# Four-tap convolutions moved from VectorE to GpSimd, and one modulation group from the input stage to the output projection

## The chip, the cores and the metric

The kernel runs on one core of a Trainium2 chip. The metric is the device time of one execution in microseconds (us); the time before is the median of three runs, 1684.27 us (1683.55 to 1684.93). Profiles come from one further execution of the same program.

The engines in the text: TensorE (PE) multiplies matrices into PSUM, VectorE (DVE), ScalarE (ACT) and GpSimd (POOL) work element by element, SyncE (SP) only issues DMAs. Each runs its own instructions in order, and they wait for each other by semaphores. All data is float32.

## What is computed

One layer of a hybrid backbone on 256 tokens and 256 context tokens of width 2048. What matters here:

```python
sh1, sc1, gt1, sh2, sc2, gt2 = adaln(c, w_mod[l], b_mod[l])     # silu(c) @ w_mod + b_mod, 6 x 2048
hx = modulate(rms_norm(x, g_mix[l]), sh1, sc1)                  # the same for the context with c_ctx
x_pool, x_u, x_v, x_lru, x_lg, x_q, x_k, x_val = jnp.split(hx @ w_in[l], 8, axis=-1)
...
def centred_depthwise_conv(z, w, b):                            # CONV_W = 4 taps, 512 channels
    zp = jnp.pad(z, ((0, 0), (left, CONV_W - 1 - left), (0, 0)))
    out = zp[:, 0:L] * w[0] + b
    for k in range(1, CONV_W):
        out = out + zp[:, k:k + L] * w[k]
    return out
...
# rg_lru: r, i = sigmoid(block-diagonal products of z), a = exp(-8 r softplus(-lam)),
# b = sqrt(1 - a^2) * i * z, a scan over the tokens, forward and backward
y_lru = (hx_f + hx_b) * gelu(x_lg)
x_mixed = x + gt1 * merge_branches(hx, [y_pool, y_sgu, y_lru, y_na], w_branch[l], w_gate[l], w_out[l])
hx2 = modulate(rms_norm(x_mixed, g_ffn[l]), sh2, sc2)
x = x_mixed + gt2 * swiglu(hx2, ...)
```

## The kernel before

**Pieces.** The large weights come in pieces of 512 KB (256 rows by 512 columns) through a ring of four buffers. For each piece SyncE issues the DMA into RAW (L274) once VectorE has done with the piece four earlier, ScalarE rounds it to HI (`high`, L428) once TensorE has done with the piece four earlier, VectorE makes the rest LO = RAW - HI (`low`, L735), and TensorE multiplies HI and LO with both parts of the activations in three passes (L1279 to L1281, in the input stage partly L1251 to L1253). A piece is 12 matmuls of 512 columns where the tokens are the rows.

**The order of the rest.** Pieces are numbered by w. ScalarE and VectorE call `high(w)` or `low(w)` and then `straight(w)`, TensorE multiplies piece w and then calls its own `straight(w)`; these hold, at fixed w, all small work of the branches. Pieces 16 to 63 belong to the input projection, 64 to 95 to the gates of the first pass, 96 to 103 to its branch products. Then a loop makes three more passes of 40 pieces, then come 32 pieces of the output projection, then the feed-forward stage.

**The recurrent branch** has four groups g at LRU_AT = 71, 77, 83, 88. For A = LRU_AT[g]: VectorE convolves at w = A - 3 (L991, L994: one tensor_scalar and three scalar_tensor_tensor over 512 columns, 256 context and 256 x tokens) from LP into one of two rows Z; TensorE makes four float32 products of Z after piece A (L1480, L1481); ScalarE takes sigmoids at A + 4 (L575, L576), tanh and exp at A + 5 (L582, L583), a square root at A + 7 (L587) and the rounded result at A + 9 (L590); VectorE works at A + 6 (L957 to L960, semaphore lru_w), at A + 8 (L966 to L979, with the scans) and at A + 10 (L820). On ScalarE a `high` stands between each two of these steps, on VectorE a `low`.

**The modulation.** The last four of the six vectors are 16 groups of 512 columns, each 16 tiles of w_mod (128 x 512, 256 KB), loaded by GpSimd's queue (L392) and added up by VectorE (`mod_tile`, L832 and L834), then turned by TensorE (`mod_turn`) and read (`mod_columns`, L841, L843). Groups 0 to 2 are early, one tile per piece at w = 24 to 71 with the two rows MR; groups 3 to 11 are in the loop, three per pass at its w = 4 to 35 with the four rows MR4; groups 12 to 15 are in the feed-forward stage. Between groups 8 and 9 GpSimd's queue loads x again (L401, two DMAs of 1 MB in rows of 8 KB). JUNK is a 512-column scratch row that lies in the attention's space and is otherwise used for squares much later.

Of the kernel before, what the change touches and what calls it, by code (L numbers as in the profile page):

```python
# [31 lines left out]
T = 256  # L32
# [61 lines left out]

MOD2_0, EARLY, MOD_TILES = 24, 3, 3 * KT
MOD_AT = [[t for t in range(MOD_TILES) if 4 + t * 32 // MOD_TILES == w] for w in range(BLK)]
# [30 lines left out]
def build(nc, x, c, ctx, c_ctx, w_mod, b_mod, g_mix, g_ffn, g_final, w_in, w_pool, pool_scale,  # L127
# [3 lines left out]
    with ctxs:  # L131
# [217 lines left out]
        def _(pool):  # L349
# [45 lines left out]
            with pool.Fori(0, EARLY) as g:  # L395
                mod_group(g, MR, 2, "mod_landed")
            pool.wait_ge(s("branches_made"), 1)
            with pool.Fori(EARLY, 9) as g:
# [326 lines left out]
        def _(dve):  # L725
# [119 lines left out]
            def straight(w):  # L845
                if MOD2_0 <= w < MOD2_0 + EARLY * KT:
                    mod_tile((w - MOD2_0) // 16, (w - MOD2_0) % 16, ACCM[:, (w - MOD2_0) // 16 % 2, :])
                if w in (47, 63):
                    mod_columns((w - 47) // 16, 0)
                if w == 20:  # L850
# [99 lines left out]
                for g in range(G4):  # L950
# [29 lines left out]
                    if w == LRU_AT[g] + 10:  # L980
                        split_low("lru_hi", g + 1, Y[:, 8 + g, 1, :], HS, Y[:, 8 + g, 0, :], "lru_lo")
                if w + 3 in LRU_AT:

                    g = LRU_AT.index(w + 3)
                    z = Z[:, g % 2, :].rearrange("p (s t) -> p s t", s=2)
                    dve.wait_ge(s("win_read"), 4)
                    if g == 0:
                        dve.wait_ge(s("pooled"), 1)
                    if g >= 2:
                        dve.wait_ge(s("lru_w"), 2 * (g - 1))  # L990
                    own.did(ts(z, LP[:, g, :, 0:T], PB[:, PB_CW + g:PB_CW + g + 1], PB[:, PB_CB + g:PB_CB + g + 1], ALU.mult, ALU.add))  # L991
                    for k in range(1, CONV):
                        own.wait()
                        i = stt(z, LP[:, g, :, k:k + T], PB[:, PB_CW + 4 * k + g:PB_CW + 4 * k + g + 1], z, ALU.mult, ALU.add)  # L994
                        if k < CONV - 1:
                            own.did(i)
                        else:
                            i.then_inc(s("conv"), 1)

            def merge(f, n, b):  # L1000
# [22 lines left out]
            dve.wait_ge(s("lru_lo"), 4)  # L1023
            own.did(dve.tensor_copy(ACCB[:, 2, :], ACCM[:, 0, :]))
            own.wait()
# [3 lines left out]
            with dve.Fori(1, 4) as f:  # L1029
                own.enter(f, 1, 3)  # L1030
                for w in range(BLK):
                    low(f * BLK + (MIX0 + w), w % 4)
                    for t in MOD_AT[w]:
                        mod_tile(f * 3 + t // KT, t % KT, ACCB[:, t // KT, :])
                    if w in MOD_READ_AT:
                        mod_columns(f * 3 + MOD_READ_AT.index(w) - 1, 4)
                    if w == 1:
                        merge(f - 1, 2, 0)
                    if w == 3:
                        merge(f - 1, 3, 2)  # L1040
                    if w == 37:
                        merge(f, 0, 0)
                    if w == 39:
                        merge(f, 1, 2)
                own.leave(1, 3)
# [26 lines left out]
            for n in range(4):  # L1072
                for j in range(8):
# [6 lines left out]
                    if 8 * n + j == 4:  # L1080
                        gate1_spread()
                    if 8 * n + j == 17:
                        mod_columns(11, 6)
                    if n and j == 3:
# [157 lines left out]
        def _(pe):  # L1242
# [175 lines left out]
            def straight(w):  # L1418
                if w in (44, 60):

                    g = (w - 44) // 16
                    pe.wait_ge(s("win_read"), (5, 7)[g])
                    mod_turn(g, ACCM[:, g % 2, :], 0)
                if w in (47, 63):
                    pe.wait_ge(s("mod_read"), (w - 31) // 16)
                if w == 34:
# [45 lines left out]
                for g in range(G4):  # L1472
                    if w == LRU_AT[g]:
                        pe.wait_ge(s("conv"), g + 1)
                        pe.wait_ge(s("pool_lo"), 4)
# [78 lines left out]
            with pe.Fori(1, 4) as f:  # L1554
                base = MIX0 + f * BLK
                for n in range(NB):
# [4 lines left out]
                    for w in gate_group(base, n):  # L1561
                        if w == MG_TURN_AT:
                            pe.wait_ge(s("mg_set"), f)
                            merged_turn(f - 1)
                        if w in MOD_TURN_AT:

                            i = MOD_TURN_AT.index(w) - 1
                            pe.wait_ge(s("mod_read"), f * 3 + i)
                            mod_turn(f * 3 + i, ACCB[:, i % 3, :], 4)
                for n in range(NB):  # L1570
# [6 lines left out]
            def gate1_spread():  # L1577

                pe.wait_ge(s("gate1_diag"), 1)
                pe.wait_ge(s("mg_lo"), 4)  # L1580
                pe.wait_ge(s("mod_read"), 11)
                for n in range(4):
# [3 lines left out]
            def xm_turn(n):  # L1586
# [4 lines left out]
                else:  # L1591
                    pe.wait_ge(s("xmt_set"), n - 1)
                if n == 1:
                    pe.wait_ge(s("mod_read"), 12)
                for k in range(4):
# [5 lines left out]
            for n in range(4):  # L1601
# [4 lines left out]
                for j in range(8):  # L1606
# [8 lines left out]
                    if 8 * n + j == 12:  # L1615
                        pe.wait_ge(s("gate1_rows"), 2)
                        mod_turn(11, ACCB[:, 2, :], 6)
                    if n and j == 3:
# [127 lines left out]
```

## Time and profile before

| | |
|---|---|
| median of three runs | 1684.27 us |
| the profiled execution | 1683.08 us |
| its span in the trace | 1681.4 us |
| mean granted clock of TensorE | 0.989 of full speed |
| PE busy | 1627.3 us (97%) |
| DVE busy | 1095.1 us (65%) |
| ACT busy | 733.1 us (44%) |
| POOL busy | 159.2 us (9%), DMA issue alone |
| DMA | 389.09 MB, 231 GB/s on average |

The page counts an engine as busy while an instruction runs. Matmuls overlap, so a busy TensorE is not one at its peak. A view of waits gives for each group of instructions how long its engine stood idle just before it, and who released it. The view in order of time gives start, duration and, in brackets, the idle time before with its releaser.

### The profile page before, as it was taken

What the parts mean: (1) busy time and instruction counts of PE and PEld (TensorE: products, weight loads), DVE (VectorE), ACT (ScalarE), POOL (GpSimd) and SP (SyncE); (2) the same over time, 40 slices, a digit from 0 to 9 for tenths busy, and PEclk for the clock granted to TensorE, in tenths of its full rate; (3) what the DMA queues carried; (4) which work ended last, traced back from release to release, by engine and by line L of the source; (5) the groups of instructions that cost most, each with busy time, mean ns of one, the idle gap of its engine ahead of it and who ended that gap; (6) DMA issues with size and microseconds to landing.
All of it is one profiled execution on the core that took longest, in us unless ns stands there. A gap on an engine that the chain in (4) does not pass through costs nothing.

```text
span 1681.4 us, 22407 instructions
## 1 busy us (share of the span) xinstructions
PE 1627.3 (97%) x7679; PEld 1321.5 (79%) x7679; DVE 1095.1 (65%) x1218; ACT 733.1 (44%) x798; POOL 159.2 (9%) x294
## 2 busy tenths in 40 slices
PE   5999999999899999999999899999999999999998
PEld 2468889987678888788878688888888888888876
DVE  2424336787788887788856657767665556456477
ACT  4324224547744434344444643444444444444434
POOL 1002011110002212222100001101100000000000
PEclk9899999999999999999999899999999999999999
DMA  9997457664369979989655468778776566666653
GB/s 354 382 366 226 138 150 226 205 218 148 125 206 330 330 261 327 334 283 332 234 187 186 137 204 277 244 236 288 230 275 194 187 193 189 191 189 188 186 163 138
DMA packets 183862, 389.09 MB, mean 231 GB/s; under 512 B 14368, under 2 KB 14608, under 8 KB 182912
## 3 DMA queue, kind: packets, MB, share of 16 engines
q1 hardware_dynamic: 160784, 312.63, 57.2%
q0 software_dynamic: 23024, 75.74, 12.9%
q8 instruction: 34, 0.56, 0.1%
q14 instruction: 20, 0.16, 0.0%
HBM read 385.30 MB, written 3.01 MB: 231 GB/s over the span
## 4 chain that ended last, share of the span: by engine, by line
PE 88%; DVE 4%; ACT 3%; DMA 3%; issue 1%; SPq 0%; DVEq 0%; ACTq 0%; POOLq 0%
PE ps L1279 24%; PE ps L1281 23%; PE ps L1280 23%; PE ps L1251 4%; PE ps L1252 4%; PE ps L1253 4%; PE ps L1247 2%; PE ps L1332 2%; ACT HI L428 1%; DVE LO L735 1%; DMA BR<-in_w_mod 1%; DMA MR<-in_w_mod 1%; DMA RAW<-in_w_branch 1%; PE ps L1441 0%; PE ps L1455 0%
## 5 line engine op out<-in xcount | busy, mean ns | idle before, releaser
L735 DVE TENSOR_TENSOR LO<-RAW,HI 128x1024 fp32r<-128x1024 f32 x504 | 616.2, 1224 | 449.3 <-ACT HI L428 446.8
L428 ACT ACTIVATE HI<-RAW 128x1024 fp32r<-128x1024 f32 x504 | 533.8, 1061 | 790.7 <-PE ps L1281 680.1
L1279 PE MATMUL ps<-HI,H 128*128 128x512 f32 x1904 | 749.9, 394 | 16.1 <-DVE LO L735 10.9
L1281 PE MATMUL ps<-HI,H 128*128 128x512 f32 x1904 | 743.7, 391 | 0.0
L1280 PE MATMUL ps<-LO,H 128*128 128x512 f32 x1904 | 743.3, 390 | 0.0
L1279 PEld LDWEIGHTS ps<-HI,H 128*128 128x128 f32 x1904 | 359.0, 189 | 96.2 <-DVE LO L735 13.1
L1281 PEld LDWEIGHTS ps<-HI,H 128*128 128x128 f32 x1904 | 358.8, 188 | 75.3
L1280 PEld LDWEIGHTS ps<-LO,H 128*128 128x128 f32 x1904 | 359.3, 189 | 74.6 <-issue 1.2
L392 POOL DMA_DIRECT2D BR<-in_w_mod x208 | 112.1, 539 | 749.5 <-DVE BR L834 329.7
L832 DVE SCALAR_TENSOR_TENSOR BR<-BR,SCF 128x512 f32<-128x512 f32 (+1 forms) x195 | 145.7, 747 | 2.8 <-DMA BR<-in_w_mod 1.4
L1251 PE MATMUL ps<-H,HI 128*128 128x256 f32 (+1 forms) x384 | 126.1, 328 | 0.0
L1252 PE MATMUL ps<-H,HI 128*128 128x256 f32 (+1 forms) x384 | 122.5, 319 | 0.0
L1253 PE MATMUL ps<-H,LO 128*128 128x256 f32 (+1 forms) x384 | 122.3, 319 | 0.0
L1251 PEld LDWEIGHTS ps<-H,HI 128*128 128x128 f32 x384 | 73.2, 191 | 21.4 <-issue 16.8
L1253 PEld LDWEIGHTS ps<-H,LO 128*128 128x128 f32 x384 | 73.1, 190 | 5.3
L1252 PEld LDWEIGHTS ps<-H,HI 128*128 128x128 f32 x384 | 73.2, 191 | 4.7
L392 POOL DMA_DIRECT2D MR<-in_w_mod x48 | 26.2, 547 | 190.1 <-DVE ACCM L832 153.3
L1138 DVE TENSOR_TENSOR ATT<-ps,ATT 128x1024 f32<-128x1024 f32 x36 | 43.8, 1218 | 0.0
L1332 PE MATMUL ps<-BR 128*32 128x512 f32 x112 | 24.4, 717 | 18.9 <-DMA BR<-in_w_mod 15.0
L832 DVE SCALAR_TENSOR_TENSOR ACCM<-MR,SCF,ACCM 128x512 f32<-128x512 f32 x45 | 33.6, 747 | 7.4 <-DMA MR<-in_w_mod 7.3
L421 ACT ACTIVATE HI<-RAW 128x1024 fp32r<-128x1024 f32 x16 | 16.8, 1054 | 42.5 <-PE ps L1253 37.9
L731 DVE TENSOR_TENSOR LO<-RAW,HI 128x1024 fp32r<-128x1024 f32 x16 | 19.4, 1223 | 19.9 <-ACT HI L421 19.7
(252 smaller groups left out, 742.3 us busy)
## 6 DMA issues: line engine op xcount, KB each, us to landing
RAW<-in_w_gate SPq DMA_DIRECT2D x128, 512.0 KB, 4.7
BR<-in_w_mod POOLq DMA_DIRECT2D x208, 256.0 KB, 4.5
RAW<-in_w_ffn_gate SPq DMA_DIRECT2D x88, 512.0 KB, 3.8
RAW<-in_w_ffn_up SPq DMA_DIRECT2D x88, 512.0 KB, 3.8
RAW<-in_w_ffn_down SPq DMA_DIRECT2D x88, 512.0 KB, 3.7
RAW<-in_w_in SPq DMA_DIRECT2D x64, 512.0 KB, 4.5
RAW<-in_w_branch SPq DMA_DIRECT2D x32, 512.0 KB, 4.9
RAW<-in_w_out SPq DMA_DIRECT2D x32, 512.0 KB, 4.0
```

What stands on the lines that cost most here:

```text
L392: pool.dma_start(slots[:, k % ring, :], w_mod[0, k * P:(k + 1) * P, bass.ds(2 * D + g * BW, BW)])\
L428: act.activation(HI[:, j % RING, :], RAW[:, j % RING, :], ACT.Copy).then_inc(hi_done, 1)
L735: tt(LO[:, j % RING, :], RAW[:, j % RING, :], HI[:, j % RING, :], ALU.subtract).then_inc(lo_done, 1)
L832: i = stt(acc, src, SCF[:, 0, k:k + 1], acc, ALU.mult, ALU.add)
L1138: tt(flat(ACC[:, n, :]), pair(4 + 2 * (n % 2)), flat(ACC[:, n, :]), ALU.add).then_inc(s("down_read"), 1)
L1251: mm(o, wh, xh, start=first, stop=False, skip_group_check=True)
L1252: mm(o, wh, xl, start=False, stop=False, skip_group_check=True)
L1253: return mm(o, wl, xh, start=False, stop=last, skip_group_check=True)
L1279: mm(o, xh, wh, start=first and t == 0, stop=False, skip_group_check=True)
L1280: mm(o, xh, wl, start=False, stop=False, skip_group_check=True)
L1281: i = mm(o, xl, wh, start=False, stop=last and t == 1, skip_group_check=True)
L1332: m = mm(ps[32 * g:32 * g + 32, 6, :], SCP[:, k, :], mod_raw(p + g // 2)[:, g % 2 * BW:(g % 2 + 1) * BW], start=i % 4 == 0, stop=i % 4 == ...
```

## The change

The convolutions leave VectorE. GpSimd does them, between the early modulation groups and the loop's: per group one tensor_scalar into Z and, for each of the other three taps, a tensor_scalar into the scratch row JUNK and a tensor_tensor that adds it to Z, seven instructions in place of four, each waiting for the one before by the semaphore conv_step. Groups 0 and 1 can run as soon as the attention and the pooling have left JUNK and Z; groups 2 and 3 wait for lru_w as before. TensorE waits for conv_step in place of conv.

EARLY goes from 3 to 2. Group 2 leaves w = 56 to 71, every group of the loop moves on by one place (2 to 10 in place of 3 to 11), and group 11 is added up during the output projection, one tile per piece at its pieces 8 to 23, turned after piece 27 and read at piece 31. The second load of x stands where it did in GpSimd's program, behind group 8, and that group is now the first of the third pass of the loop (the last of the second before).

```diff
-MOD2_0, EARLY, MOD_TILES = 24, 3, 3 * KT
+MOD2_0, EARLY, MOD_TILES = 24, 2, 3 * KT
...
@@ block.gpsimd, between the early and the later groups of w_mod @@
             with pool.Fori(0, EARLY) as g:
                 mod_group(g, MR, 2, "mod_landed")
+
+            def convolve(g):
+
+                z = Z[:, g % 2, :].rearrange("p (s t) -> p s t", s=2)
+                if g == 0:
+                    pool.wait_ge(s("win_read"), 4)
+                    pool.wait_ge(s("params"), 1)
+                    pool.wait_ge(s("pooled"), 1)
+                    pool.wait_ge(s("att_out"), 4)
+                if g >= 2:
+                    pool.wait_ge(s("lru_w"), 2 * (g - 1))
+                pool.tensor_scalar(z, LP[:, g, :, 0:T], PB[:, PB_CW + g:PB_CW + g + 1], PB[:, PB_CB + g:PB_CB + g + 1],
+                                   ALU.mult, ALU.add).then_inc(s("conv_step"), 1)
+                tap = JUNK.rearrange("p (s t) -> p s t", s=2)
+                for k in range(1, CONV):
+                    pool.wait_ge(s("conv_step"), 7 * g + 2 * k - 1)
+                    pool.tensor_scalar(tap, LP[:, g, :, k:k + T], PB[:, PB_CW + 4 * k + g:PB_CW + 4 * k + g + 1], None, ALU.mult)                        .then_inc(s("conv_step"), 1)
+                    pool.wait_ge(s("conv_step"), 7 * g + 2 * k)
+                    pool.tensor_tensor(z, z, tap, ALU.add).then_inc(s("conv_step"), 1)
+
+            for g in range(G4):
+                convolve(g)
             pool.wait_ge(s("branches_made"), 1)
@@ block.vector, straight(w) @@
-                if w in (47, 63):
-                    mod_columns((w - 47) // 16, 0)
+                if w == 47:
+                    mod_columns(0, 0)
...
-                if w + 3 in LRU_AT:
-
-                    g = LRU_AT.index(w + 3)
-                    z = Z[:, g % 2, :].rearrange("p (s t) -> p s t", s=2)
-                    dve.wait_ge(s("win_read"), 4)
-                    if g == 0:
-                        dve.wait_ge(s("pooled"), 1)
-                    if g >= 2:
-                        dve.wait_ge(s("lru_w"), 2 * (g - 1))
-                    own.did(ts(z, LP[:, g, :, 0:T], PB[:, PB_CW + g:PB_CW + g + 1], PB[:, PB_CB + g:PB_CB + g + 1], ALU.mult, ALU.add))
-                    for k in range(1, CONV):
-                        own.wait()
-                        i = stt(z, LP[:, g, :, k:k + T], PB[:, PB_CW + 4 * k + g:PB_CW + 4 * k + g + 1], z, ALU.mult, ALU.add)
-                        if k < CONV - 1:
-                            own.did(i)
-                        else:
-                            i.then_inc(s("conv"), 1)
@@ block.vector, after the first pass and in the merge loop @@
-            own.did(dve.tensor_copy(ACCB[:, 2, :], ACCM[:, 0, :]))
+            own.did(dve.tensor_copy(ACCB[:, 2, :], ACCM[:, 1, :]))
...
-                        mod_tile(f * 3 + t // KT, t % KT, ACCB[:, t // KT, :])
+                        mod_tile(f * 3 + (t // KT - 1), t % KT, ACCB[:, t // KT, :])
...
-                        mod_columns(f * 3 + MOD_READ_AT.index(w) - 1, 4)
+                        mod_columns(f * 3 + (MOD_READ_AT.index(w) - 2), 4)
@@ block.vector, output projection @@
                     if 8 * n + j == 17:
+                        mod_columns(10, 6)
+                    if 8 <= 8 * n + j < 24:
+                        mod_tile(11, 8 * n + j - 8, ACCB[:, 0, :])
+                    if 8 * n + j == 31:
                         mod_columns(11, 6)
@@ block.tensor @@
-                if w in (44, 60):
-
-                    g = (w - 44) // 16
-                    pe.wait_ge(s("win_read"), (5, 7)[g])
-                    mod_turn(g, ACCM[:, g % 2, :], 0)
-                if w in (47, 63):
-                    pe.wait_ge(s("mod_read"), (w - 31) // 16)
+                if w == 44:
+
+                    pe.wait_ge(s("win_read"), 5)
+                    mod_turn(0, ACCM[:, 0, :], 0)
+                if w == 47:
+                    pe.wait_ge(s("mod_read"), 1)
...
-                        pe.wait_ge(s("conv"), g + 1)
+                        pe.wait_ge(s("conv_step"), 7 * (g + 1))
...
-                            pe.wait_ge(s("mod_read"), f * 3 + i)
-                            mod_turn(f * 3 + i, ACCB[:, i % 3, :], 4)
+                            pe.wait_ge(s("mod_read"), f * 3 + (i - 1))
+                            mod_turn(f * 3 + (i - 1), ACCB[:, i % 3, :], 4)
...
-                pe.wait_ge(s("mod_read"), 11)
+                pe.wait_ge(s("mod_read"), 10)
...
                 if n == 1:
+                    pe.wait_ge(s("mod_read"), 11)
+                if n == 3:
                     pe.wait_ge(s("mod_read"), 12)
...
-                        mod_turn(11, ACCB[:, 2, :], 6)
+                        mod_turn(10, ACCB[:, 2, :], 6)
+                    if 8 * n + j == 27:
+                        pe.wait_ge(s("xmt_set"), 2)
+                        mod_turn(11, ACCB[:, 0, :], 6)

```

## Rows read from the trace of the kernel before

**Rows 1.** The page, part 1: busy us, share of the span, instructions.

```profile
PE 1627.3 (97%) x7679; PEld 1321.5 (79%) x7679; DVE 1095.1 (65%) x1218; ACT 733.1 (44%) x798; POOL 159.2 (9%) x294
```

**Rows 2.** What TensorE waited for in the whole span: us in total, times, longest.

```profile
PE ps L1279 <- DVE LO L735: 10.9, 10, 3.6
...
PE ps L1279 <- DVE ATT L1008: 1.8, 1, 1.8
```

**Rows 3.** Busy time of each engine in a stretch of the recurrent stage.

```profile
core 0: us, PE busy (x) PEld busy (x) DVE busy (x) ACT busy (x) POOL busy (x), PEclk, DMA share, GB/s
...
430.00:440.00 10.00, 7.40 (x27) 6.00 (x28) 5.68 (x7) 9.95 (x13) 0.00 (x0) 0.83 0.47 157
```

**Rows 4.** TensorE in order of time, recurrent stage: start, us, instruction, idle before.

```profile
417.04 0.50 PE L1279 MATMUL ps<-HI,H 128*128 128x512 f32 x1 [0.39 <-DVE LO L735]
...
419.90 1.02 PE L1480 MATMUL ps<-BR 128*128 128x512 f32 x2
...
432.60 0.79 PE L1279 MATMUL ps<-HI,H 128*128 128x512 f32 x1 [3.62 <-DVE LO L735]
...
442.23 1.02 PE L1480 MATMUL ps<-BR 128*128 128x512 f32 x2
...
474.95 0.50 PE L1279 MATMUL ps<-HI,H 128*128 128x512 f32 x1 [2.01 <-DVE LO L735]
```

**Rows 5.** ScalarE in order of time, recurrent stage.

```profile
386.06 1.06 ACT L428 ACTIVATE HI<-RAW 128x1024 fp32r<-128x1024 f32 x1 [0.64 <-PE ps L1281]
...
404.86 0.42 ACT L590 ACTIVATE H<-BR 128x256 fp32r<-128x256 f32 x1 [5.22 <-DVE BR L979]
...
414.69 1.04 ACT L428 ACTIVATE HI<-RAW 128x1024 fp32r<-128x1024 f32 x1
```

**Rows 6.** VectorE in order of time, recurrent stage (one earlier row, gelu).

```profile
367.09 0.69 DVE L927 TENSOR_SCALAR ATT<-ATT 128x1024 f32<-128x1024 f32 x1
...
396.99 1.22 DVE L735 TENSOR_TENSOR LO<-RAW,HI 128x1024 fp32r<-128x1024 f32 x1
...
404.40 0.43 DVE L979 TENSOR_TENSOR BR<-BR 128x256 f32<-128x256 f32 x1
...
406.45 2.33 DVE L994 SCALAR_TENSOR_TENSOR BR<-BR,PB 128x512 f32<-128x512 f32 x3
...
415.77 1.22 DVE L735 TENSOR_TENSOR LO<-RAW,HI 128x1024 fp32r<-128x1024 f32 x1 [3.60 <-ACT HI L428]
...
429.09 2.33 DVE L994 SCALAR_TENSOR_TENSOR BR<-BR,PB 128x512 f32<-128x512 f32 x3
431.33 2.35 DVE L735 TENSOR_TENSOR LO<-RAW,HI 128x1024 fp32r<-128x1024 f32 x2
...
439.53 1.23 DVE L735 TENSOR_TENSOR LO<-RAW,HI 128x1024 fp32r<-128x1024 f32 x1 [3.60 <-ACT HI L428]
```

**Rows 7.** Groups between 370 and 480 us: line, shapes, count, busy us, mean ns.

```profile
L994 DVE SCALAR_TENSOR_TENSOR BR<-BR,PB 128x512 f32<-128x512 f32 x9 | 6.8, 752 | 0.3
...
L957 DVE TENSOR_TENSOR ATT<-ATT,BR 128x512 f32<-128x512 f32 x8 | 5.5, 684 | 0.0
...
L991 DVE TENSOR_SCALAR BR<-BR,PB 128x512 f32<-128x512 f32 x3 | 1.6, 543 | 0.0
```

**Rows 8.** The second load of x (L401) from issue to landing.

```profile
DMA to landing us min/median/max: 8.5/10.0/11.4
```

**Rows 9.** Waits between 680 and 850 us.

```profile
ACT HI L428 <- DMA RAW<-in_w_branch: 7.7, 3, 5.3
```

**Rows 10.** GpSimd, then VectorE in order of time, third pass of the loop.

```profile
749.76 1.13 POOL L392 DMA_DIRECT2D BR<-in_w_mod  x2 [0.52 <-issue]
...
754.66 0.48 DVE L834 TENSOR_SCALAR BR<-BR,SCF 128x512 f32<-128x512 f32 x1
```

**Rows 11.** Busy time in a stretch of the output projection (columns as in Rows 3).

```profile
880.00:900.00 20.00, 20.00 (x94) 16.60 (x93) 14.38 (x14) 9.68 (x12) 0.00 (x0) 1.00 0.53 185
```

**Rows 12.** VectorE in order of time, end of the output projection.

```profile
919.70 1.23 DVE L735 TENSOR_TENSOR LO<-RAW,HI 128x1024 fp32r<-128x1024 f32 x1 [2.31 <-ACT HI L428]
```

## The prediction

> **What bounds the kernel now.** I read the page's busy times first: TensorE is busy for 97% of the span [rows 1], so time can be won only where it waits, and can be lost wherever another engine becomes late. The waits on TensorE over the whole span come next: 10.9 us behind VectorE's LO in ten places, the longest 3.6, and 1.8 us behind a merge (L1008) [rows 2]. Most of the 10.9 lie in the recurrent stage, where in one stretch of 10 us TensorE is busy for 7.40 at a mean granted clock of 0.83 while ScalarE is busy for 9.95 [rows 3]. So this is the only part of the input stage that the change can speed up, and the question is what ends last there.
>
> The order of time of the three engines answers it. LO of piece 83 starts at 415.77 and LO of piece 89 at 439.53, both after 3.60 us idle behind ScalarE's HI [rows 6]: 23.8 us for the six pieces of one group. TensorE needs less for them: piece 83 starts at 417.04 and its recurrent products at 419.90, 2.9 us for a piece, and four products of about 1.02 [rows 4], so 6 x 2.9 + 4.1 = 21.5 us at most. The stage is bound by a loop through ScalarE and VectorE. Followed back from 415.77: HI of piece 83 at 414.69 is the end of unbroken ScalarE work that began at 404.86 with L590, and L590 had waited 5.22 us for VectorE's L979 [rows 5], which started at 404.40 as the last of nine instructions from 396.99 on [rows 6]. The loop is: VectorE's A+6 work, ScalarE's roots, VectorE's A+8 work to L979, ScalarE's L590, sigmoids, tanh and exp, the next HI, and A+6 again.
>
> **What the change removes.** The convolutions of groups 2 and 3 stand at 406.45 and 429.09 on VectorE [rows 6], after L979, beside the ScalarE part of the loop. Each costs 0.54 + 3 x 0.75 = 2.8 us [rows 7]. The first is followed by 3.60 us of idle VectorE at 415.77: taken away, that idle time grows and piece 83 comes no sooner. The second delays LO of piece 86, which starts at 431.33 [rows 6], and TensorE waits 3.62 us until 432.60 for it [rows 4]. Taken away, that wait falls to 3.6 - 2.8 = 0.8 us. But the loop does not pass through it: LO of piece 89 still starts at 439.53 behind ScalarE, and TensorE, now 2.8 us earlier, meets the loop again some pieces later; its last wait there, 2.01 us to 474.95 [rows 4], is for a piece that comes no sooner. I value the removal at 0. The convolutions of groups 0 and 1, and the 16 modulation tiles of about 0.75 us each (12 us; the same kind and size as a tap [rows 7]) all lie before 386.06, where ScalarE is waiting for TensorE and not for VectorE [rows 5]: what is won on VectorE before this point is lost to the ring of four pieces. Value 0 too. What is late next, if these go, is TensorE's own work, unchanged. The early turn of a modulation group by TensorE (four transposes) goes and comes back after piece 27 of the output projection: 0.
>
> **What it adds on GpSimd.** Seven instructions a group, four with one input and three with two. No row shows GpSimd computing; its instructions in the trace are DMA issues. The nearest rows are VectorE's: one input of 512 columns 0.54 us, two inputs 0.68 us [rows 7]. A floor is 4 x 0.54 + 3 x 0.68 = 4.2 us a group. Above, I take the 1.22 us of the 1,024-column LO [rows 6] for all seven, 8.5 us. I take 0.6 and 1.2, nearer the floor for the simple ones: 6.0 us a group, an estimate. By its own speed this is hidden: group 2 can start when lru_w rises, at 397.0, and is wanted at 419.90; group 3 a loop later, at 397.0 + 23.8 = 420.8, and wanted at 442.23 [rows 4], 21 us for 6. Queued behind it on GpSimd is nothing but the wait for branches_made.
>
> What isn't hidden, in my forecast, is the neighbour. Both late convolutions start at once after lru_w, and so run exactly beside the nine VectorE instructions from 396.99 to 404.83 (LO of two pieces and the A+8 work) and their like a group later. These are on the loop, and all have two inputs in SBUF. A one-input instruction over 1,024 columns takes 0.69 us where LO with two inputs takes 1.22 [rows 6]: VectorE needs all its read paths for two inputs, and a neighbour that shares one stands in the way. The trace shows no such pair, so the bounds are 0 (no interference) and full alternation: each of the seven GpSimd instructions delays one of the nine by its own length. That gives 6.0 us less some 0.5 us of idle time inside the block, 5.5 us, and for two groups 11.0 us (2 x (4.2 - 0.5) = 7.4 to 2 x (8.5 - 0.5) = 16). I take the upper case, since the block has almost no gaps and both engines are ready at the same time. Groups 0 and 1 cost nothing either way: they run before the reset at 386.06, beside 17 us that VectorE has just been given.
>
> The Trainium skill says in "SBUF — State Buffer", section "Who interferes with whom", that a VectorE instruction with two SBUF inputs contends with a GpSimd instruction that reads SBUF, by an exclusive lock for the whole instruction. By that rule the term is the 11.0 us of the alternation, without it 0. The Trainium skill's "GPSIMD Engine Reference", section 3.1, gives 4,497 ns for a two-input add over 2048 columns and 769 ns for a simple loop over 512; by these, an estimate, a group takes 3 x 1.1 + 4 x 0.77 = 6.4 us. Nothing in this trace shows either.
>
> **What it moves.** The second load of x goes out behind group 8, now in the third pass, about where a tile's DMA goes out at 749.76 [rows 10]. It took 8.5 to 11.4 us to land [rows 8]. Before, it delayed a branch piece so that ScalarE waited 5.3 us [rows 9] and TensorE 1.8 [rows 2]; that is won. Now the next group's tiles queue behind it and can't land before 749.8 + 11.4 = 761.2, while VectorE wants the first at 754.66 [rows 10]. It stands still for 6.5 us with its LO behind it. The tile and the next LO (0.75 + 1.22) follow, 8.5 us in all. TensorE is covered by the pieces made ahead, up to three of 2.9 us less one HI and one LO (1.06 [rows 5] + 1.22), 6.4 us; it waits for 2.1 us. Net +0.3 us, between -1.8 (all hidden) and +4 (the weights late as well).
>
> Group 11 in the output projection adds 16 x 0.75 = 12 us to VectorE over 16 pieces, 16 x 2.9 = 46 us. The fullest 20 us there have 5.6 us free [rows 11], so 46 us have at least 12.9. The 256 KB a piece more is less than the loop's. Cost 0; if the cover is gone 1 to 2 us. Its reading at piece 31, one instruction over 512 columns and a short one, under 1 us, lies in the 2.31 us idle before 919.70 [rows 12]; 0.
>
> **The sum.** 1683.1 (this execution, of which the span is 1681.4) + 11.0 + 0.3 = 1694.4 us. The median of three is 1.2 us above the execution: 1695.6. Its own range: 1684.3 + 7.4 - 1.8 = 1690 to 1684.3 + 16 + 4 = 1704.
>
> **The rivals.** (1) No interference worth the name: both late convolutions run beside the block for free. 1684.3 + 0.3 = 1684.6, within 0.2%. For it: 21 us of room for each convolution, so GpSimd may take every wait itself. Against: the block and the convolutions start together. (2) Faster: the 2.8 us taken from in front of piece 86 are kept instead of being given back. It needs ScalarE's part of the loop to move up with TensorE, for which nothing speaks in the order of time; it would bring -2.8, about -1.7 for the half-clock stretch behind the 3.62 us wait (0.17 of 10 us [rows 3]), and -1.8 if the x load hides: 1678. (3) GpSimd itself is the bound: from 3.0 us an instruction on, seven exceed the 21 us between lru_w and TensorE's demand. At 4 us they take 28, TensorE waits 5 and 7 us: 1696 without interference, over 1704 with it.
>
> **Chances.** Forecast 0.50; rival 1 0.28; rival 2 0.14; rival 3 0.05; 0.03 for an output projection or an x load that costs more by itself. A difference of 0.2% (3.4 us) is about what a measurement of this kernel can tell from no change. Rival 2 is the faster case (0.14, and 0.01 from rival 1's edge), rival 1 the same (0.27), the rest slower (0.58). That the change does something else than it says can't be: the diff holds all of it. The range runs from 1681, below rival 1, to 1705, the end of the forecast's own.
>
> **What would show it.** Right: VectorE's instructions between lru_w and L979 stretched or with gaps, L979 of group 0 near 410 instead of 404.4, ScalarE's wait before L590 near 10.7 us instead of 5.22, a TensorE wait of about 6 us before piece 83. Rival 1: L979 at 404.4 and 3.6 us or more idle before LO of pieces 83 and 89, no wait left at piece 86 but new ones before 93. Rival 3: TensorE waiting for GpSimd before L1480. The x load: an idle VectorE behind a tile near 755. Wrong altogether, if LO of piece 89 comes clearly before 439.

## The result and the profile after

The changed kernel takes 1687.42 us (median of 17 runs, 1685.39 to 1689.53) where the kernel before took 1684.27 in the same series: a ratio of 1.0019, 95% interval [1.0012, 1.0025], or 3.2 us more. It is slower, but by less than a third of the 11.3 us forecast. It lies inside the wide range of 1681 to 1705 us and outside the forecast's own range of 1690 to 1704, and it is nearer to rival 1 (1684.6, no interference) than to the forecast (1695.6). The profiled execution took 1688.18 us, its span 1686.5, at a mean granted clock of 0.987; it lies 5.1 us over that of before, so its rows show a little more than the medians do. One of the 10 executions of experiment 4 took 5817.69 us, for which no cause is on record; its ratio below leaves it out, and without it the median there is 1680.94 in place of 1681.03.

In the changed kernel VectorE's LO stands on L757 (L735 before), ScalarE's HI on L450 (L428), lru_w's last on L982 (L960), the A+8 work on L988 to L1001 (L966 to L979), the rounded result on L612 (L590). The page, part 1, answers [rows 1]:

```profile
PE 1630.3 (97%) x7679; PEld 1322.0 (78%) x7679; DVE 1096.0 (65%) x1202; ACT 733.2 (43%) x798; POOL 212.6 (13%) x322
```

GpSimd is busy for 53 us more, and VectorE for as long as before, although it has lost 11 us of convolutions (4 x 2.8). The waits of TensorE over the span answer [rows 2] (us in total, times, longest):

```profile
PE ps L1287 <- DVE LO L757: 14.8, 15, 2.0
```

Waits for LO have grown from 10.9 to 14.8 us, in 15 shorter pieces in place of 10; the 1.8 us behind the merge are gone. The stage is told by VectorE in order of time (start, us, instruction, idle before), which answers [rows 6]:

```profile
392.56 1.22 DVE L757 TENSOR_TENSOR LO<-RAW,HI 128x1024 fp32r<-128x1024 f32 x1 [3.61 <-ACT HI L450]
...
397.56 1.22 DVE L757 TENSOR_TENSOR LO<-RAW,HI 128x1024 fp32r<-128x1024 f32 x1
399.29 1.22 DVE L757 TENSOR_TENSOR LO<-RAW,HI 128x1024 fp32r<-128x1024 f32 x1 [0.51 <-ACT HI L450]
400.43 0.68 DVE L988 TENSOR_TENSOR ATT<-ATT 128x512 f32<-128x512 f32 x1
401.15 1.51 DVE L990 TENSOR_TENSOR_SCAN ATT<-ATT 128x512 f32<-128x512 f32 x1
402.58 1.78 DVE L988 TENSOR_TENSOR ATT<-ATT 128x512 f32<-128x512 f32 x1
404.39 1.07 DVE L992 TENSOR_TENSOR_SCAN ATT<-ATT 128x256 f32<-128x256 f32 x1
405.50 0.75 DVE L995 TENSOR_TENSOR_SCAN ATT<-ATT 128x256 f32<-128x256 f32 x1
406.28 1.33 DVE L1000 TENSOR_TENSOR BR<-ATT 128x256 f32<-128x256 f32 x1
407.65 0.80 DVE L1001 TENSOR_TENSOR BR<-BR 128x256 f32<-128x256 f32 x1
...
419.38 1.23 DVE L757 TENSOR_TENSOR LO<-RAW,HI 128x1024 fp32r<-128x1024 f32 x1 [3.59 <-ACT HI L450]
...
445.71 1.23 DVE L757 TENSOR_TENSOR LO<-RAW,HI 128x1024 fp32r<-128x1024 f32 x1 [3.60 <-ACT HI L450]
```

These are the nine instructions ("the block" from here on), with LO of pieces 77, 83 and 89 around them. The block lasts from 397.56 to 408.45, 10.9 us; before it took 396.99 to 404.83, 7.8 us [rows 6]. Four rows of before, LO of piece 77, the scan, the second of the two L966 (L988 now) and L978 (L1000 now):

```profile
391.99 1.23 DVE L735 TENSOR_TENSOR LO<-RAW,HI 128x1024 fp32r<-128x1024 f32 x1 [3.60 <-ACT HI L428]
...
400.58 1.23 DVE L968 TENSOR_TENSOR_SCAN ATT<-ATT 128x512 f32<-128x512 f32 x1
401.73 0.67 DVE L966 TENSOR_TENSOR ATT<-ATT 128x512 f32<-128x512 f32 x1
...
403.94 0.43 DVE L978 TENSOR_TENSOR BR<-ATT 128x256 f32<-128x256 f32 x1
```

Not all nine are longer: the scan L990 by 0.3 us, the second L988 by 1.1 (the first, 0.68, is undisturbed), L1000 by 0.9, L992 and L1001 by 0.4 each. From LO of piece 77 to that of 83 it is 26.82 us and to that of 89 another 26.33; before, the two steps were 23.78 and 23.76 (from 391.99 on, with [rows 6]). So 3.0 and 2.6 us were lost, 5.6 in all. GpSimd beside it, group 2:

```profile
397.75 1.67 POOL L408 TENSOR_SCALAR BR<-BR,PB 128x512 f32<-128x512 f32 x1 [13.13 <-DVE ATT L982]
399.51 2.95 POOL L413 TENSOR_SCALAR ATT<-BR,PB 128x512 f32<-128x512 f32 x1
402.54 1.27 POOL L415 TENSOR_TENSOR BR<-BR,ATT 128x512 f32<-128x512 f32 x1
403.91 1.89 POOL L413 TENSOR_SCALAR ATT<-BR,PB 128x512 f32<-128x512 f32 x1
405.88 1.45 POOL L415 TENSOR_TENSOR BR<-BR,ATT 128x512 f32<-128x512 f32 x1
407.43 1.61 POOL L413 TENSOR_SCALAR ATT<-BR,PB 128x512 f32<-128x512 f32 x1
409.13 1.60 POOL L415 TENSOR_TENSOR BR<-BR,ATT 128x512 f32<-128x512 f32 x1
```

From the first start to the last end it is 13.0 us, not 6.0. GpSimd is slowed more than it slows: the same L408 took 0.76 us at 355.41, and here 1.67. ScalarE and TensorE, in order of time, answer [rows 5] and [rows 4]:

```profile
408.48 0.42 ACT L612 ACTIVATE H<-BR 128x256 fp32r<-128x256 f32 x1 [8.28 <-DVE BR L1001]
```

```profile
420.66 0.50 PE L1287 MATMUL ps<-HI,H 128*128 128x512 f32 x1 [1.80 <-DVE LO L757]
...
435.98 0.50 PE L1287 MATMUL ps<-HI,H 128*128 128x512 f32 x1 [1.77 <-DVE LO L757]
```

ScalarE's wait grew from 5.22 to 8.28 us, the block's 3.0. TensorE waits 1.80 us for piece 83 (0.39 before [rows 4]) and 1.77 us for piece 86, where it waited 3.62.

The other two places. Behind the load of x, VectorE stands still for the next tile (first row) and TensorE has no wait there. In the output projection group 11 costs VectorE busy time (second row: 18.24 us of 20 against 14.38 [rows 11], columns as in [rows 3]) and costs TensorE nothing, which is busy for all 20:

```profile
762.65 0.49 DVE L856 TENSOR_SCALAR BR<-BR,SCF 128x512 f32<-128x512 f32 x1 [4.59 <-DMA BR<-in_w_mod]
```

```profile
880.00:900.00 20.00, 20.00 (x94) 16.62 (x93) 18.24 (x21) 9.70 (x13) 3.42 (x7) 1.00 0.77 258
```

### The profile page after: what moved, and what is told of

It reads as the page before. It is cut to its first block, busy times and chain, and to the rows that moved or that the text cites. A ratio compares the mean times of both kernels' runs of the same rounds, so it can differ in the third digit from the quotient of the medians.

```text
span 1686.5 us, 22419 instructions
## 1 busy us (share of the span) xinstructions
PE 1630.3 (97%) x7679; PEld 1322.0 (78%) x7679; DVE 1096.0 (65%) x1202; ACT 733.2 (43%) x798; POOL 212.6 (13%) x322
## 4 chain that ended last, share of the span: by engine, by line
PE 89%; DVE 4%; ACT 3%; DMA 2%; issue 1%; SPq 0%; DVEq 0%; ACTq 0%
PE ps L1287 24%; PE ps L1289 24%; PE ps L1288 24%; PE ps L1259 4%; PE ps L1261 4%; PE ps L1260 4%; PE ps L1255 2%; PE ps L1340 2%; ACT HI L450 1%; DMA MR<-in_w_mod 1%; DVE LO L757 1%; DMA BR<-in_w_mod 1%; PE ps L1448 0%; PE ps L1462 0%; DVE ATT L988 0%
## 5 line engine op out<-in xcount | busy, mean ns | idle before, releaser
L757 DVE TENSOR_TENSOR LO<-RAW,HI 128x1024 fp32r<-128x1024 f32 x504 | 621.0, 1234 | 441.7 <-ACT HI L450 439.9
L450 ACT ACTIVATE HI<-RAW 128x1024 fp32r<-128x1024 f32 x504 | 533.7, 1060 | 792.7 <-PE ps L1289 678.5
L1287 PE MATMUL ps<-HI,H 128*128 128x512 f32 x1904 | 750.3, 394 | 18.8 <-DVE LO L757 14.8
L392 POOL DMA_DIRECT2D BR<-in_w_mod x224 | 120.3, 537 | 672.1 <-DVE BR L854 317.5
L854 DVE SCALAR_TENSOR_TENSOR BR<-BR,SCF 128x512 f32<-128x512 f32 (+1 forms) x210 | 156.7, 746 | 10.9 <-DMA BR<-in_w_mod 9.9
L392 POOL DMA_DIRECT2D MR<-in_w_mod x32 | 17.4, 545 | 139.5 <-DVE ACCM L854 105.5
L1255 PEld LDWEIGHTS ps<-CST,BR 128*128 128x128 f32 (+1 forms) x177 | 22.0, 150 | 12.2 <-DMA CST<-in_cst 4.0
```

The costliest lines, as they stand in the source:

```text
L392: pool.dma_start(slots[:, k % ring, :], w_mod[0, k * P:(k + 1) * P, bass.ds(2 * D + g * BW, BW)])\
L450: act.activation(HI[:, j % RING, :], RAW[:, j % RING, :], ACT.Copy).then_inc(hi_done, 1)
L757: tt(LO[:, j % RING, :], RAW[:, j % RING, :], HI[:, j % RING, :], ALU.subtract).then_inc(lo_done, 1)
L854: i = stt(acc, src, SCF[:, 0, k:k + 1], acc, ALU.mult, ALU.add)
L1255: return mm(o, src, IDENT[0:n, 0:n], start=start, stop=True, is_transpose=True, skip_group_check=True)
L1287: mm(o, xh, wh, start=first and t == 0, stop=False, skip_group_check=True)
```

## The experiments

Times of one series are compared with the runs of the kernel before in it. Each edit is against the kernel that it names.

**1. The convolutions alone.** The kernel before, with `convolve` on GpSimd behind its three early groups (EARLY stays 3) and no convolution on VectorE.

```diff
             with pool.Fori(0, EARLY) as g:
                 mod_group(g, MR, 2, "mod_landed")
...
+            for g in range(G4):
+                convolve(g)
```

> The convolutions alone on GpSimd, the modulation groups as in the kernel before. Theory (interference on the loop): the nine VectorE instructions from the LO after lru_w to the end of the A+8 work last about 10.7 us in place of 7.8 for groups 0 and 1, LO of piece 89 comes some 5.6 us later than in the kernel before, and the time is 4.5 to 6 us over it, about 1689.5, more than the change as a whole costs, since the 1.8 us at the branch products are not won. Rival (the moved group or the moved x load is what costs): 1684 to 1685, as before.

Measured: 1692.80 us, ratio 1.0047 [1.0033, 1.0061], 8.8 us over before (1683.99), some 3 us more than expected. The convolutions alone cost more than the whole change. The profiled execution took 1696.74 us, 3.9 more than the median, and a tile's DMA that goes out at 340.29 in the rows of before goes out at 343.57 in it; so steps and waits are read from it, not starts. The interference is the same (LO of pieces 77, 83, 89 at 399.61, 426.42, 452.74: steps of 26.8 and 26.3), but now group 0 starts late, in GpSimd's order of time:

```profile
368.93 0.54 POOL L392 DMA_DIRECT2D MR<-in_w_mod  x1 [2.84 <-DVE ACCM L853]
369.60 1.21 POOL L407 TENSOR_SCALAR BR<-BR,PB 128x512 f32<-128x512 f32 x1
```

This is 14 us later than in the changed kernel (355.41), some 3 of which stand before any convolution. What TensorE waits for has a new entry, at 385.47, before group 0's products:

```profile
PE ps L1483 <- POOL BR L414: 3.0, 1, 3.0
```

GpSimd works through its program in order: L407 starts right behind the last DMA issue of early group 2 (368.93). That with the move groups 0 and 1 cost nothing fits this. This run also leaves the 16 tiles of group 2 on VectorE, so the earlier start and the unburdened VectorE are not told apart.

**2. The move alone.** The changed kernel with the convolutions put back on VectorE at A - 3.

```diff
-            for g in range(G4):
-                convolve(g)
...
+                if w + 3 in LRU_AT:
```

> The modulation group and with it the x load moved as in the change, the convolutions left on VectorE. Theory: the loop in the recurrent stage is as before, LO of piece 89 at 439 to 440, TensorE's wait of 1.8 us before the merge is gone and nothing replaces it: about 1682.5, 1.5 to 2 us under the kernel before. Rival (the moved group is what costs): 1687 or more.

Measured: 1681.32 us, ratio 0.9983 [0.9974, 0.9992], 2.7 us under before (1.5 to 2 were expected). LO of piece 89 comes 47.55 us after that of 77 (47.54 before), so the recurrent stage is the old one:

```profile
392.84 1.23 DVE L736 TENSOR_TENSOR LO<-RAW,HI 128x1024 fp32r<-128x1024 f32 x1 [3.60 <-ACT HI L429]
...
440.39 1.23 DVE L736 TENSOR_TENSOR LO<-RAW,HI 128x1024 fp32r<-128x1024 f32 x1 [3.59 <-ACT HI L429]
```

The move wins 2.7, and the convolutions on top of it cost 6.1 (1687.42 - 1681.32, two series with nearly equal times before).

**3. Late convolutions started behind the block.** The changed kernel; groups 2 and 3 wait for the end of the nine instructions.

```diff
                 if g >= 2:
-                    pool.wait_ge(s("lru_w"), 2 * (g - 1))
+                    pool.wait_ge(s("lru_float"), g - 1)
```

> The changed kernel, but the convolutions of groups 2 and 3 wait for lru_float, that is for VectorE's last A+8 instruction, in place of lru_w. The same work on the same engine, started where the loop is in ScalarE's part. Theory: the nine instructions are back at 7.8 us, the seven GpSimd instructions are shorter (about 8 to 9 us together in place of 13 to 14), LO of piece 89 is at 439 to 440 and the time about 1682.5, as with the move alone. Rival (GpSimd's own length is what costs, so a later start can only hurt): TensorE waits before L1488's products for conv_step, 1688 to 1692.

Measured: 1683.76 us, ratio 1.0001 [0.9992, 1.0010]. The block is back at 7.8 us (397.57 to 405.41), and 3.7 of the 6.1 us are won. The rest stays for two reasons. GpSimd still needs 12 us and now meets three LOs; the last of them, LO of piece 83 itself, is stretched, on the loop, and before group 3's products TensorE waits for the convolution:

```profile
416.35 2.16 DVE L757 TENSOR_TENSOR LO<-RAW,HI 128x1024 fp32r<-128x1024 f32 x1 [3.14 <-ACT HI L450]
...
441.05 2.13 DVE L757 TENSOR_TENSOR LO<-RAW,HI 128x1024 fp32r<-128x1024 f32 x1 [3.15 <-ACT HI L450]
```

```profile
PE ps L1487 <- POOL BR L415: 1.1, 1, 1.1
```

The step from piece 83 to piece 89 is 24.7 instead of 23.8, 0.9 us for a LO that is 0.9 too long; the step before it is still 23.8 (from 392.57).

**4. The same seven writes without reads.** The changed kernel; the late groups' instructions are fills of the same rows, so their convolution isn't computed.

```diff
+                if g >= 2:
+                    pool.memset(z, 0.01).then_inc(s("conv_step"), 1)
+                    for k in range(1, CONV):
+                        pool.wait_ge(s("conv_step"), 7 * g + 2 * k - 1)
+                        pool.memset(tap, 0.01).then_inc(s("conv_step"), 1)
+                        pool.wait_ge(s("conv_step"), 7 * g + 2 * k)
+                        pool.memset(z, 0.01).then_inc(s("conv_step"), 1)
+                    return
```

> The changed kernel, but the 14 GpSimd instructions of groups 2 and 3 are replaced by fills of the same rows with a constant, in the same chain of waits: the convolutions of these two groups are left out. Theory (what is shared is the reading of SBUF): VectorE's nine instructions are at 7.8 us again though GpSimd is busy beside them, and the time is about 1682.5. Rival (any GpSimd instruction beside VectorE delays it, by its semaphores or its writes): the block stays near 10 us where the fills overlap it, 1685 to 1688.

Measured: 1681.03 us, ratio 0.9982 [0.9972, 0.9991], the same as the move alone. The fills run at one pace in the first 4 us of the block (GpSimd in order of time, the first of seven equal ones), and no VectorE instruction is longer than before:

```profile
396.37 0.53 POOL L410 MEMSET BR<- 128x512 f32 x1 [13.04 <-DVE ATT L990]
```

So the price is not for GpSimd's writes, its semaphores or its place. That it is for the reads follows only in part: a fill is also shorter than what it replaces, and no run has a GpSimd instruction that lasts as long without reading SBUF. And since here VectorE has neither convolutions nor interference, their removal is worth 0.3 to 0.4 us against experiment 2 (the intervals allow about 1 either way). TensorE's wait for piece 86 falls to the 0.8 us that the prediction named:

```profile
429.02 0.50 PE L1295 MATMUL ps<-HI,H 128*128 128x512 f32 x1 [0.80 <-DVE LO L765]
```

**5. and 6. Which instructions.** The late groups keep only the three adds (the four others are fills), or only the four one-input instructions (the adds are fills); either way the late convolution isn't computed.

The edit of scales_only; adds_only has the same one at the tensor_scalars of z and tap.

```diff
-                    pool.tensor_tensor(z, z, tap, ALU.add).then_inc(s("conv_step"), 1)
+                    if g < 2:
+                        pool.tensor_tensor(z, z, tap, ALU.add).then_inc(s("conv_step"), 1)
+                    else:
+                        pool.memset(z, 0.01).then_inc(s("conv_step"), 1)
```

> The changed kernel, but of the seven GpSimd instructions of groups 2 and 3 only the three two-input additions are left; the four with one input are fills of the same rows (their part of the convolution is left out). If each GpSimd instruction that reads delays VectorE by its own length (my price), the nine instructions last 7.8 + 3 x 1.3 = 11.7 us and the loss stays above the change's. If only the time in which both want to read counts, and fills are free, they last 8.5 to 9.5 us, and LO of piece 89 comes 1.5 to 3 us after the 440.4 of the move alone.

> The counterpart: the four one-input instructions of groups 2 and 3 stay on GpSimd, the three additions are fills (left out). By the price of its own length (1.6 us each as seen) the block would last 7.8 + 6.4 = 14 us; by the time shared it lasts 9 to 10 us. Together with the run before it, the two parts should make up the 3.0 us that all seven cost; if the parts make much more, GpSimd's instructions hold each other back and not VectorE.

Measured, adds: 1687.30 us, 1.0018 [1.0009, 1.0028]; scales: 1684.37, 0.9999 [0.9990, 1.0009], both against 1684.34. In the first, VectorE's block takes 10.7 us (+2.9), between the two values that the expectation named (11.7, and 8.5 to 9.5). All of it is in three instructions (VectorE, then GpSimd's three adds in order of time):

```profile
397.93 1.98 DVE L763 TENSOR_TENSOR LO<-RAW,HI 128x1024 fp32r<-128x1024 f32 x1 [0.51 <-ACT HI L456]
399.83 1.75 DVE L994 TENSOR_TENSOR ATT<-ATT 128x512 f32<-128x512 f32 x1
...
402.76 1.72 DVE L994 TENSOR_TENSOR ATT<-ATT 128x512 f32<-128x512 f32 x1
```

```profile
397.53 1.30 POOL L421 TENSOR_TENSOR BR<-BR,ATT 128x512 f32<-128x512 f32 x1
...
399.49 1.54 POOL L421 TENSOR_TENSOR BR<-BR,ATT 128x512 f32<-128x512 f32 x1
...
401.69 2.23 POOL L421 TENSOR_TENSOR BR<-BR,ATT 128x512 f32<-128x512 f32 x1
```

Three adds, three VectorE instructions longer by 0.75, 1.07 and 1.05: one for one. The rows also say why these sizes. Each of the three starts while an add is under way, and at that moment the add has 0.90, 1.20 and 1.16 us left (it ends at 398.83, 401.03 and 403.92). Each is longer by this rest less 0.11 to 0.15. In the second the block takes 8.9 us (+1.1; 9 to 10 were expected), also with three longer ones (0.3, 0.4, 0.4), and it is GpSimd that is held up (two of its instructions, then VectorE's and GpSimd's in the last of the three meetings):

```profile
397.02 1.67 POOL L408 TENSOR_SCALAR BR<-BR,PB 128x512 f32<-128x512 f32 x1 [13.09 <-DVE ATT L985]
398.77 2.95 POOL L413 TENSOR_SCALAR ATT<-BR,PB 128x512 f32<-128x512 f32 x1
```

```profile
404.92 0.80 DVE L1004 TENSOR_TENSOR BR<-BR 128x256 f32<-128x256 f32 x1
```

```profile
404.66 1.67 POOL L413 TENSOR_SCALAR ATT<-BR,PB 128x512 f32<-128x512 f32 x1
```

L1004 starts when the one-input instruction has 1.41 us left, and is longer by 0.4: the rest less 1.0, in all three meetings. From LO of piece 77 to that of 89 it is 53.30 us and 49.66 us, against 47.54 and 47.55 without interference (before, experiment 2): 5.8 and 2.1.

**7. The load of x behind group 11.** The kernel before; only the place of the load changes.

```diff
-            with pool.Fori(EARLY, 9) as g:
+            with pool.Fori(EARLY, 12) as g:
...
-            with pool.Fori(9, 16) as g:
+            with pool.Fori(12, 16) as g:
```

> The kernel before with one edit: the second load of x goes out behind group 11, at the end of the last pass of the merge loop, where no tile is needed soon and the weights' share of the DMA is low. It shares only this edit's effect with the change. Theory (the whole gain of the move is TensorE's wait of 1.8 us at the branch products behind the x load): that wait goes, nothing takes its place, 1.8 to 2.7 us under the kernel before. Rival (the gain of the move came from the 12 us of tiles taken from the input stage, and the x load was hidden anyway): as before, within 0.5 us.

Measured: 1685.20 us, ratio 1.0002 [0.9992, 1.0012]; the expectation missed. The load lands in 8.7 to 11.6 us, in front of the branch weights of the last pass, and the waits are the old ones a pass later (first ScalarE, 680 to 960 us, then TensorE, whole span):

```profile
ACT HI L428 <- DMA RAW<-in_w_branch: 8.4, 3, 5.6
```

```profile
PE ps L1279 <- DVE ATT L1008: 2.1, 1, 2.1
```

So moving the load is not enough. In front of branch weights it costs the wait, here and before; amid the tiles of a pass, as in the change, it does not.

**8. HI ahead of the rounded result.** The kernel of experiment 2; ScalarE splits the next piece before L590's copy of the result (groups 0, 1 and 3), VectorE's part one piece later.

```diff
-                    if w == LRU_AT[g] + 9:
+                    if w == LRU_AT[g] + (9 if g == 2 else 10):
...
-                    if w == LRU_AT[g] + 10:
+                    if w == LRU_AT[g] + (10 if g == 2 else 11):
```

> Built on the move alone (convolutions on VectorE): for groups 0, 1 and 3 ScalarE makes HI of the next piece before it waits for VectorE's A+8 work (L590 at A+10 in place of A+9, VectorE's LO of it at A+11). If the loop through ScalarE and VectorE is what ends last, it gets shorter by one HI, 1.0 us, for each of groups 0 and 1: LO of piece 89 near 438.4 in place of 440.4, and the time 2 to 3 us under the move alone, about 1679. Rival (TensorE or VectorE alone bounds the stage): no change against the move alone, 1681.3.

Measured: 1679.17 us, ratio 0.9971 [0.9959, 0.9983], 5.2 us under before and the fastest kernel here. ScalarE in order of time has three HI behind one another where the third used to wait behind the block:

```profile
398.10 3.08 ACT L429 ACTIVATE HI<-RAW 128x1024 fp32r<-128x1024 f32 x3
405.31 0.42 ACT L591 ACTIVATE H<-BR 128x256 fp32r<-128x256 f32 x1 [4.13 <-DVE BR L980]
```

LO of pieces 77, 83 and 89 stand at 392.44, 415.26 and 438.07: steps of 22.8, one HI (1.04) less than 23.8. It shows the loop for what it was taken to be.

**9. The same with the convolutions on GpSimd.** The changed kernel with the edit of experiment 8.

> The changed kernel (convolutions on GpSimd, the group moved) with the reordering of the run before: ScalarE makes HI of the next piece ahead of L590's rounded result, for groups 0, 1 and 3. Is the price of GpSimd's late convolutions a constant that is added to whatever the loop is? The convolutions themselves do not move: they still start at lru_w, beside the same nine instructions. Theory (the loop goes through the block in either order): +6.1 us over the same kernel with the convolutions on VectorE (1679.2), so 1685.3 (1684.3 to 1686.3), the block 3.0 us longer, and LO of piece 89 some 5.7 us later after LO of piece 77 than there (45.6), so 51.3. Rival (with HI made ahead, ScalarE waits less for the end of the block and part of the delay falls into slack): 1681 to 1683, LO of piece 89 within 49 us of LO of piece 77.

Measured: 1684.53 us, ratio 0.9998 [0.9989, 1.0007], 5.4 us over experiment 8, or 4.5 us by the two ratios, since the time before is 0.6 us higher in this series. LO of pieces 77, 83, 89:

```profile
392.10 1.22 DVE L757 TENSOR_TENSOR LO<-RAW,HI 128x1024 fp32r<-128x1024 f32 x1 [3.60 <-ACT HI L450]
...
417.49 1.23 DVE L757 TENSOR_TENSOR LO<-RAW,HI 128x1024 fp32r<-128x1024 f32 x1 [3.26 <-ACT HI L450]
...
442.87 1.22 DVE L757 TENSOR_TENSOR LO<-RAW,HI 128x1024 fp32r<-128x1024 f32 x1 [3.26 <-ACT HI L450]
```

Steps of 25.4 against 22.8, 2.6 a group. The price comes on top of the shorter loop too; none of it falls into slack. (LO of piece 89 comes 50.8 us after 77, not the 51.3 expected: the first block also loses only 2.6 here, the pairs falling a little differently.)

## Why the prediction was half right

**The bound and the loop: right.** LO of pieces 83 and 89 still starts after 3.6 us of idle VectorE behind ScalarE's HI, and each microsecond put into the block (experiments 5, 6, 9) or taken out of ScalarE's part (8) came out between these LOs.

**Removal worth nothing: right.** The fills and the move alone differ by 0.3 to 0.4 us. The 3.62 us wait at piece 86 fell to 0.80 with the fills, as forecast, and to 1.77 in the changed kernel, whose block is longer; waits of 0.4 to 2.0 us elsewhere took its place, as the loop demands. Rival 2, which kept this gain, is out; rival 1 by the blocks; rival 3 too, for TensorE waits for GpSimd only in experiments 1 (3.0 us) and 3 (1.1 us), where the convolutions start later.

**The interference: the mechanism right, its size wrong; this is the step that failed.** The prediction put "each of the seven GpSimd instructions delays one of the nine by its own length", 5.5 us a group. Measured: the block grew by 3.0 and 2.6 us, and so did the loop. Two errors partly cancel. The length was underrated: an add takes 1.27 us at best (1.2 was taken), a one-input instruction 0.76 at best and mostly 1.6 to 3.5 (0.6 was taken). And the delay was overrated, for two reasons that the rows show.

First, a VectorE instruction never waits for the whole of its neighbour, but for what is left of it. Under an add it is longer by the rest less 0.11 to 0.15 us, in all twelve such meetings in the late groups of experiment 5 and of the changed kernel (L988 at 402.58: the add ends at 403.81, 1.23 us on, and L988 is longer by 1.11). Under a one-input instruction it is the rest less 1.0 to 1.1 in experiment 6 and in the changed kernel, which leaves 0.4 or less and often nothing. Experiment 3 has up to 0.5, and one kind of meeting (LO at 406.84 under L408) in which it is the rest, 0.35, less 0.15.

Second, alternation was taken as one-sided, with all the waiting on VectorE; in fact GpSimd does most of it: its seven instructions last 13.0 us, against 6.9 at their best durations (3 x 1.27 + 4 x 0.76). In group 3 the first add starts just ahead of L988 and it is the add that waits, 1.85 us in place of 1.27, while L988 is undisturbed:

```profile
429.37 1.85 POOL L415 TENSOR_TENSOR BR<-BR,ATT 128x512 f32<-128x512 f32 x1
```

```profile
429.40 0.66 DVE L988 TENSOR_TENSOR ATT<-ATT 128x512 f32<-128x512 f32 x1
```

So only nine of the fourteen instructions lengthened a block. In group 2 these are two adds (1.1 and 0.9, at L988 and L1000) and three one-input instructions (0.3 to 0.4, at L990, L992, L1001), together 3.0; the third add starts at 409.13, behind the block. In group 3 they are two and two, together 2.6. Alone, adds and one-input instructions cost the block 2.9 + 1.1 = 4.0 us. Together it is 3.0, one add less.

The bounds of 7.4 to 16 us for both groups did not hold the 5.6 measured. The lower one took VectorE's durations as a floor for GpSimd's and full alternation as certain; a price between "none" and "full" had no case of its own. The Trainium skill, "SBUF — State Buffer", "Who interferes with whom", has an exclusive lock for a whole instruction that blocks whichever engine comes second; 11 us came out of it only because the prediction let VectorE be second every time, and for the neighbour's whole length. The runs agree for the adds, in either order, and for the fills (0.53 us each, VectorE undisturbed). They do not for most meetings with the one-input instructions, where VectorE goes on 1.0 us before the recorded end of the neighbour.

**What it cost in time: as much as the loop says.** The forecast's check points were L979 of group 0 at 410 (its answer, L1001, ran at 407.65), ScalarE's wait at 10.7 (8.28) and a TensorE wait of 6 before piece 83 (0.42 at 415.84, then 1.80 at 420.66): pieces made ahead covered more of the smaller delay.

**Group 0 and 1 at nothing: right, with a condition not seen.** The forecast named the removed VectorE work as their cover. Experiment 1 shows that their place on GpSimd's queue matters as well: behind one more early group they start later, TensorE waits 3.0 us for group 0, and the convolutions cost 8.8 us instead of 6.1. The 3.0 us are about the 2.7 between these two; how much of them the tiles left on VectorE make was not tested.

**The move: the mechanism half right.** The 1.8 us behind the merge went, as forecast. The 2.1 us expected in its place did not come: the load landed in 8.0 to 8.3 us and not 11.4, VectorE stood still for 4.59 us and not 6.5, and the pieces made ahead held. Forecast +0.3, measured -2.7 [-4.4, -1.3] for the move as a whole (experiment 2); 1.8 of this has a row, 0.9 has none and is within the interval. Whether the tiles taken from the input stage have a part in it was not tested; LO of piece 77 came no earlier without them (392.84 in experiment 2, 391.99 before). Experiment 7 shows that the gain hangs on the place. The output projection cost nothing, as said.

**The sum.** 2 x 2.8 for the blocks less 1.8 for x is +3.8 on 1684.3; the residual add that ends the output projection comes at 930.45 against 926.71 before, +3.7 in the profiled executions, and the medians say +3.2. The forecast had 11.0 + 0.3. Against the runs, the first term was too high by 4.9 us (6.1 measured for the convolutions) and the second by 3.0 (-2.7 for the move): both errors lie on the same side and did not cancel.

## What to carry over

Moving work off a busy engine wins only what lies on the path, and here nothing did; what it costs is set by what runs beside it in its new place, so look for the window in which the neighbour's two-input instructions stand, above all on the loop that sets the pace. Price interference between none and full, with a case for each, since both engines give way: an instruction pays at most for what is left of its neighbour when it starts. An engine's queue is a place too: a step that is moved onto it starts behind all that is issued ahead of it. When a stage is a loop, shorten the loop: one activation taken out of it (experiment 8) won 2.1 us, where the offloading of the convolutions lost 6.1.

## What the runs showed of the hardware

- GpSimd instructions that read SBUF and VectorE instructions with two inputs there hold each other up, and one at a time. Under a GpSimd add over 512 columns (1.27 to 1.60 us in most places, up to 2.4) a VectorE instruction is longer by the rest of the add less 0.11 to 0.15 us, at most 1.1; under a one-input tensor_scalar mostly by its rest less 1.0, at most 0.5. When VectorE is first, GpSimd waits, and the one-input instruction suffers most: 0.76 us at its best, 3.47 at its worst in the changed kernel.
- A fill of 512 columns takes GpSimd 0.53 us beside the LOs and two-input instructions of the block, and lengthens none of them (experiment 4).
- Two loads of 1 MB, in rows of 8 KB, in front of 512 KB weight loads make ScalarE wait up to 5.3 to 5.6 us for one of these [rows 9]; amid the tiles the longest such wait was 2.9 us, though there were more of them (12.4 us in seven, against 7.7 in three).
